# Feature stages: the first two pairs of a unit as two wide and two narrow products

## What is computed

```python
def conv_ffn(x, w_in, w_dw, w_out):
    u = causal_dwconv(x @ w_in, w_dw)          # w_in: 2048 x 11264
    g, up = jnp.split(u, 2, axis=-1)
    return (jax.nn.silu(g) * up) @ w_out       # w_out: 5632 x 2048

def diff_attention(x, w_qkv, ...):
    q, k, v = jnp.split(x @ w_qkv, 3, axis=-1) # w_qkv: 2048 x 6144
    ...

for i in range(DEPTH):                         # DEPTH = 2
    h = h + rms_norm(mixer(rms_norm(h)))
    h = h + rms_norm(conv_ffn(rms_norm(h), ffn_w_in[i], ffn_w_dw[i], ffn_w_out[i]))
    h = h + per_layer_embed(h, p[i], ...)
```

## Time and profile before

| what | value |
|---|---|
| median of three runs | 2442.08 us (2440.27 to 2444.92) |
| the profiled execution | 2444.93 us |
| its span, first to last instruction | 2443.1 us |
| TensorE busy | 2399.7 us, 98% |
| VectorE busy | 1641.5 us, 67% |
| ScalarE busy | 1237.7 us, 51% |
| share of the chain on TensorE | 91% |
| mean granted clock | 0.994 |

### The profile page before, as it was taken

How to read it: one execution, slowest core, us unless ns; L and a number is a source line. 1 busy time by engine, 2 the same in 40 slices (tenths; PEclk the granted TensorE clock), 3 DMA queues, 4 the chain that set the end, 5 groups by cost and what they waited for, 6 DMA issues and landing times.

```text
span 2443.1 us, 38673 instructions
## 1 busy us (share of the span) xinstructions
PE 2399.7 (98%) x12300; PEld 2055.2 (84%) x12300; DVE 1641.5 (67%) x2224; ACT 1237.7 (51%) x1773; POOL 33.3 (1%) x61
## 2 busy tenths in 40 slices
PE   9999999999999999999899999999999999999997
PEld 8888778888888888888788887888888888888886
DVE  5999767777777754456655676577777777544465
ACT  3433655555555544356544455465656565444463
POOL 2000000000000000000000000000000000000000
PEclk9999999999999999999999999999999999999999
DMA  8552446656665565556465544646566656655564
GB/s 260 164 168 87 155 147 203 189 181 191 196 188 181 191 214 191 195 183 229 126 226 186 181 152 143 196 156 187 183 188 197 189 182 187 212 194 194 192 216 138
DMA packets 365778, 448.17 MB, mean 183 GB/s; under 512 B 27172, under 2 KB 275110, under 8 KB 364544
## 3 DMA queue, kind: packets, MB, share of 16 engines
q1 hardware_dynamic: 363568, 436.33, 56.1%
q0 software_dynamic: 2128, 10.82, 1.4%
HBM read 444.95 MB, written 2.10 MB: 183 GB/s over the span
## 4 chain that ended last, share of the span: by engine, by line
PE 91%; issue 4%; DVE 2%; ACT 1%; DMA 1%; SPq 0%; POOL 0%; DVEq 0%; ACTq 0%; POOLq 0%
PE ps L1484 31%; PE ps L1486 16%; PE ps L1519 11%; PE ps L1520 11%; PE ps L1521 11%; PE ps L1564 9%; PE ps L1464 1%; DMA gain<-in_post_ffn_g 1%; PE ps L1686 0%; PE ps L1700 0%; DMA wg<-in_conv_w_pw 0%; ACT w_hi L576 0%; DVE h L972 0%; DVE w_lo L927 0%; SPq L449 0%
## 5 line engine op out<-in xcount | busy, mean ns | idle before, releaser
L927 DVE TENSOR_TENSOR w_lo<-raw,w_hi 128x1024 fp32r<-128x1024 f32 x760 | 925.7, 1224 | 644.3 <-ACT w_hi L576 624.0
L576 ACT CAST w_hi<-raw 128x1024 fp32r<-128x1024 f32 x760 | 792.7, 1049 | 744.7 <-PE ps L1521 376.2
L1484 PE MATMUL ps<-x,w_hi 128*128 128x512 f32 x3328 | 1160.6, 394 | 3.0 <-issue 3.0
L1486 PE MATMUL ps<-x,w_lo 128*128 128x256 f32 x3328 | 928.9, 279 | 0.0
L1484 PEld LDWEIGHTS ps<-x,w_hi 128*128 128x128 f32 x3328 | 624.5, 188 | 147.0 <-issue 4.0
L1486 PEld LDWEIGHTS ps<-x,w_lo 128*128 128x128 f32 x3328 | 628.2, 189 | 0.0
L1519 PE MATMUL ps<-w_hi,mid 128*128 128x512 f32 x704 | 274.1, 389 | 3.1 <-DVE w_lo L927 3.1
L1520 PE MATMUL ps<-w_lo,mid 128*128 128x512 f32 x704 | 273.9, 389 | 0.0
L1521 PE MATMUL ps<-w_hi,mid 128*128 128x512 f32 x704 | 273.9, 389 | 0.0
L1519 PE MATMUL ps<-w_hi,x 128*128 128x512 f32 x640 | 253.4, 396 | 4.0 <-DVE x L1136 2.8
L1520 PE MATMUL ps<-w_lo,x 128*128 128x512 f32 x640 | 249.8, 390 | 0.0
(11 more groups left out here) (174 smaller groups left out, 1284.4 us busy)
## 6 DMA issues: line engine op xcount, KB each, us to landing
raw<-in_ffn_w_in SPq DMA_DIRECT2D x704, 256.0 KB, 3.1
raw<-in_ffn_w_out SPq DMA_DIRECT2D x352, 256.0 KB, 3.4
raw<-in_attn_w_qkv SPq DMA_DIRECT2D x192, 256.0 KB, 2.9
wg<-in_conv_w_pw SPq DMA_DIRECT2D x128, 256.0 KB, 3.8
raw<-in_ple_w_gate SPq DMA_DIRECT2D x128, 256.0 KB, 3.7
raw<-in_conv_w_pw SPq DMA_DIRECT2D x64, 256.0 KB, 3.6
raw<-in_attn_w_o SPq DMA_DIRECT2D x64, 256.0 KB, 3.4
raw<-in_ple_w_proj SPq DMA_DIRECT2D x16, 256.0 KB, 3.4
```

The lines of the kernel that those rows point to most:

```text
L576: nc.scalar.copy(w_hi[:, u % RING], raw[:, u % RING]).then_inc(hi_split, 1)
L927: nc.vector.tensor_tensor(w_lo[:, u % RING], raw[:, u % RING], w_hi[:, u % RING].bitcast(F32), ALU.subtract).then_inc(split_done, 1)
L1484: mm(ps[:, 4 * s + f], w_hi[:, u % RING, q, columns], x[:, kt].rearrange("p a t -> p (a t)"), start=kt == 0, stop=False)
L1486: ins = mm(ps[:, 4 * s + f, 0:T], w_lo[:, u % RING, q, columns], x[:, kt, 0], start=False, stop=kt == KT - 1)
```

## The change

The loop over `q` and `f` is written with two helpers, `wide` and `narrow`. The list `order` holds the pairs in the same order as before. The first two pairs of a call are issued as wide, wide, narrow, narrow; the rest in turn as before. Which banks are written, which product carries `start`, and which one `stop`, are as before, and so are the waits and the signal after the last product.

```diff
--- before.py
+++ after.py
@@ -1477,14 +1477,24 @@
 
                     u = place[name] + n * UPC + j
                     pe.wait_ge(split_done, plus(i, per, is_split(u)))
-                    for q in range(UNIT_KT):
-                        kt = UNIT_KT * j + q
-                        for f in blocks:
-                            columns = slice(P * f, P * (f + 1))
-                            mm(ps[:, 4 * s + f], w_hi[:, u % RING, q, columns], x[:, kt].rearrange("p a t -> p (a t)"),
-                               start=kt == 0, stop=False)
-                            ins = mm(ps[:, 4 * s + f, 0:T], w_lo[:, u % RING, q, columns], x[:, kt, 0],
-                                     start=False, stop=kt == KT - 1)
+                    def wide(q, f):
+                        kt, columns = UNIT_KT * j + q, slice(P * f, P * (f + 1))
+                        return mm(ps[:, 4 * s + f], w_hi[:, u % RING, q, columns], x[:, kt].rearrange("p a t -> p (a t)"),
+                                  start=kt == 0, stop=False)
+
+                    def narrow(q, f):
+                        kt, columns = UNIT_KT * j + q, slice(P * f, P * (f + 1))
+                        return mm(ps[:, 4 * s + f, 0:T], w_lo[:, u % RING, q, columns], x[:, kt, 0],
+                                  start=False, stop=kt == KT - 1)
+
+                    order = [(q, f) for q in range(UNIT_KT) for f in blocks]
+                    wide(*order[0])
+                    wide(*order[1])
+                    narrow(*order[0])
+                    ins = narrow(*order[1])
+                    for at in order[2:]:
+                        wide(*at)
+                        ins = narrow(*at)
                     return ins
 
                 pe.wait_ge(set_free, c + (sets_before[name] + 1))
```

## The result

The changed kernel takes 2454.36 us (median of 5 runs, 2453.48 to 2454.74), beside 2442.08 for the kernel before, now over 5 runs (2440.27 to 2446.27). The ratio is 1.0042, with a 95% interval of 1.0031 to 1.0053: slower by over 0.2%. I had forecast 2440.5, no measurable change. The time lies in the range, but the direction is that of rival B, to which I gave 0.24 (0.31 for all that is measurably slower).

What follows compares the result with a forecast made beforehand. TensorE's matmul spacing was taken to bound the feature stages. From the median 2442.08 us, 0 for the groups and none to all of qk's -3.1 us gave 2442.1 to 2439.0; forecast 2440.5, range 2434 to 2457.

Steps and rivals of the forecast that it cites:

- rival B: Units' alternate pairs behind the group run in the slow rhythm: +18.5 us at most, +13.9 for six pairs alone; chance 0.24.
- What bounds the kernel: Feature-stage loops: nothing releases TensorE late; only the spacing between matmul starts sets time and can change.
- part 3: Narrow-to-narrow spacing in each group: 120 ns, sum zero; ends -10 ns (-4.2 us) and +13 ns (+5.6 us) over 422 calls.
- rival A: Narrow products in a row close up to the short end: -4.2 us, 2434.8 or 2437.9 us; chance 0.26.
- What a product costs: Each product carries 13.3 ns beside its columns: 226.7 wide, 120 narrow; cost goes with the product, not its neighbour.
- part 5: Each unit starts anew: qk loop gives back 3.1 us, the other loops stay in the quick rhythm.
- quick rhythm: Up-stage loops: one wide and one narrow product take 346.7 ns a pair, unbroken through the loop.
- slow rhythm: Loop of the qk stage: one wide and one narrow product take 353.3 ns a pair, unbroken through the loop.
- likeliest case: Whole kernel: forecast of no measurable change, 2439 to 2442.1 us; chance 0.40 together with D.
- D: Whole kernel: the group passes unnoticed and each stage keeps its rhythm, 2442.1 us; chance 0.40 together with the forecast.
- Rival C: The group itself costs +13 ns, 5.6 us in all, the rest is quick: 2444.6 to 2447.7 us; chance 0.10.
- The base: Starting time: median of three runs, 2442.08 us, spread 4.65 us, about one qk stage in one rhythm or the other.

Runs made afterwards that it cites:

- eight and eight: Against the kernel before: each unit issues eight wide products, then eight narrow ones, instead of in turn; 2451.76 us, ratio 1.0026.

## Why the prediction was wrong

1. **What bounds the kernel**: right. TensorE's spacing in the loops moved, beside the clock at the starts of stages, and TensorE's waits stand as before (13.6 us for the new `h` against 13.4, the largest).

2. **The group of four, part 3**: nearly right. I took 0 ns, with ends of -10 and +13. Measured are +3.3 ns, which is 1.3 us over 392 loop units. In a longer row of narrow products the spacing is 120 ns as worked out. In a group of two the first narrow spacing is 113 to 116 and the second 112 to 120, which by itself would have read as rival A, but the two wide ones ahead are 230 to 236, 3 to 9 ns longer than the 226.7 of the earlier trace rows. "What a product costs" had concluded, since 226.7 + 120 gives the quick pair, that cost goes with the product and not with its neighbour. The sum is right and the conclusion isn't: in the starts a quick pair is about 230 and 117 ns, and in eight and eight the same wide product takes from 236 down to 226 by its place. The 109 ns that the prediction set beside its 120 are not borne out either. By the Trainium skill, "TensorE: Matmul & The Clock Gate", section "Back-to-back issue gap", that formula is for a single matmul by itself, and in a stream of weight loads and matmuls both set the spacing. This kernel is such a stream, and its 226.7 ns for 512 columns stand over the formula's 216.

3. **The rhythm, part 5**: this is the step that failed. I wrote that a group that sums to the quick time needs no stretching, and took quick rhythm for all loops. The group is 3.3 ns off, and the alternate pairs behind it are slow in each second unit: 40 ns for six pairs, or 20 a unit. 392 units x 23.3 = 9.1 us over all-quick loops, less the 3.0 that qk had in the slow rhythm before: +6.2, as in the table. The rhythm was in rows 5 and 9, and so was the fact that a start decides it; I had no reason for quick after a start, with slow and quick starts side by side in the earlier trace rows, and should have put the likeliest case between. (The quick start at 1615 us there stands behind the small product of line 1471, not behind transposes.) What a group does to the rhythm is given above, by the pair ahead of it. Why the engine has two rhythms and turns at these points stays open.

4. **Rival B**: right that the six alternate pairs behind the group run in the slow rhythm, and right in its price for them, 40 ns a unit. The share of units was a half, over the quarter from which I said that it decides. Its reason is not shown: it wanted a load that ends late under the first narrow product, but that product's spacing is 113 to 116 ns and not long, four groups a unit cost 13.4 ns in all, and with 224 columns the narrow spacing fell still further.

5. **Rivals A and D** are out by the eight-and-eight kernel and by the table. **Rival C** exists at a quarter of its price.

6. **The base**: I scaled by the median of three runs and supposed qk's rhythm behind their spread. Two traces of before show the same rhythms. Over the sets of runs taken beside the experiments the kernel before had medians of 2445.3, 2444.5 and 2445.1, and the changed kernel's ratio of 1.0042 is some 10 us. The loops explain 6.2 of that, or of the 8.75 us between the two profiled executions; 2 of these are clock. The rest of the difference of medians may be clock too, which isn't shown: the changed kernel's five runs have a mean granted clock of 0.990 to 0.992, the kernel before 0.991 to 0.995 beside the experiments, and three of its four runs at 0.995 are its shortest, 2439.56 to 2440.35 us.

## What to carry to other kernels

On an engine that never waits, an instruction's price can depend on the point in a repeating pattern at which it falls. Read starts and not durations, over several repetitions, and count instructions in equal windows to find loops that run the same code at two speeds. An order that interrupts a steady pattern in each round is to be judged by what the pattern does behind it. Before a difference between two variants is put down to the edit, look at the state that the edit found: the same swap gave one loop the slow and another the quick rhythm.

## What was not expected of the hardware

Alternating matmuls of 512 and 256 columns, each with its own 128-column weight load, run at 346.7 or at 353.3 ns a pair at the full clock. Either goes on for 168 units, 466 or 475 us, and a single exchange of two instructions ahead of the loop turned the one into the other. Which pair stands ahead of a group of two decides what follows it: behind the slow rhythm's pair of 241 and 120 ns it stays slow (197 of 197), behind its other two it turns quick (400 of 400), and behind quick pairs it turns slow (414 of 415). Two wide and two narrow products repeated without end have one speed, 696.7 ns for the four. Matmuls of one kind in a row settle at their columns plus 13.3 ns, and the first five or so wide ones behind narrow ones take 1 to 10 ns more (eight and eight). With 224 columns the narrow spacing fell to 101 to 109 ns, and the wide one grew from about 230 to between 238 and 245.
